# Block inversion of a chunked DeltaNet as a side chain on GpSimd, the gate-sum row in the decay buffer, norms by squares

## The chip, the cores and the metric

The kernel runs on one core of a Trainium2 chip. The metric is the device time of one execution in microseconds, as the median of several runs.

## The reference, cut to what matters

A decoder layer over 16 meta tokens and 512 positions, D = 2048, all float32:

```
xn = rmsnorm(h); proj = xn @ w_in                       # 2048 x 14368
u, z_pool, q, k, v, z, b, a, gate_pool, gate_dn = split(proj)
y_pool = (trailing_means(u) - u) @ mix * scale * silu(z_pool)
q, k, v = silu(causal_conv4(q, k, v)); q = l2norm(q) / sqrt(128); k = l2norm(k)   # 16 heads of 128
per head, chunks of C positions, decay[c, s] = exp(gcum[c] - gcum[s]) for s <= c:
    L = strict_lower(beta * (k @ k.T) * decay);  T = inverse(I + L)
    u_c = T @ (v * beta);  w_c = T @ (k * beta * exp(gcum));  qk = lower(q @ k.T * decay)
    for each chunk:  v_new = u_c - w_c @ S;  o = (q * exp(gcum)) @ S + qk @ v_new
                     S = S * g_last + (k * decay_to_end).T @ v_new
y_dn = rmsnorm(o) * silu(z)
merged = sigmoid(gate_pool) * (y_pool @ w_pool_out) + sigmoid(gate_dn) * (y_dn @ w_dn_out)
out = rmsnorm(h + merged @ w_o), meta positions dropped
```

## The kernel before, in words

**The projection** is the bulk. It is made in blocks of 256 output columns: 8 for the pooling branch, then 4 for each of 8 pairs of heads (k, q, v, z), then 16 for the merge gates. A block is a Strassen product of seven (`ORDER`), each cut in two chunks, so 14 chunks of 12 matmuls (`block_products`, L701); a float32 product is three float32r terms (high times high, high times low, low times high). For each chunk, in a ring of four slots, ScalarE copies the rounded weights (`split_hi`: `wh`, L1026) and VectorE subtracts to get the rest (`split_lo`: `wl`, L1475), three chunks ahead of TensorE (`AHEAD`). VectorE also makes four weight sums a block (`s1` to `s4`; `s2`, L1486, adds slots RE and RF and is made at chunk step t = 0 of its block), evicts the product sums (`c21`, `c22` at L1531, `c11`) and convolves. SyncE loads the weights: `block_loads` issues slots RA, RC, RF and RB of the next block, RF when VectorE has finished chunk 10 of this one. TensorE's last product in a block waits for `c22`, its last but one for `c21`.

**The side work.** While pair p is projected, the DeltaNet of pair d = p - 1 is run in between: `delta(d, m)`, 53 steps, one at each of certain hooks inside the blocks (`delta_step`: step m sits at hook 15*m//8 of the pair's 112, 28 a block). Each engine runs its own part of a step in its own instruction order, so a wait inside a step holds the projection work behind it on that engine. Named steps: G0 = 3 (Gram products of k into PSUM banks `pg`), F0 = 5 (Gram times decay into `mk`), V0 = 9 (transposes of v), W0 = 14 (inversion), L0 = 29 (blocks of the inverse are merged by matmuls), R0 = 35 (recurrence over four chunks of 128), O0 = 47 (normalise, transpose, gate). All loops over pairs are hardware loops (`Fori`) on TensorE, ScalarE, VectorE and GpSimd.

**The parts that the change touches.**
- Row load: GpSimd waits until the pair's output has been stored from `zst` (the same memory as `tm`; L2180), loads the cumulative gate row spread over 128 partitions into `tm` (L2164, L2166), subtracts each position's own sum into `dec` (L2175, L2176); VectorE then caps it (L1807) and ScalarE takes the exponential (L1189).
- Norms of k: VectorE multiplies the Gram banks by the identity into `st` (L1813, L1816), reduces (L1819, L1820), ScalarE takes the root (L1193). Norms of q: eight TensorE transposes of q into PSUM bank `pt` in two rounds (W0 + 2, W0 + 4), ScalarE squares with an accumulator (L1216).
- Inversion: `mk` (512 KB) is scaled (L1836; it is then complete, `mk_ready`), stored to DRAM (L1196, L1197), its 66 diagonal blocks of 16 x 16 come back one to a partition in `st` (L1219); VectorE inverts them by 14 steps of two dependent operations over 14 to 56 elements (L1855, L1858), copies a transposed form (L1861); two stores (L1224), and three loads bring block-diagonal matrices back into `tm` and `st` (L1227 to L1229). These DMAs are issued by ScalarE at fixed steps. TensorE's step L0 waits for `tm_loaded`.
- `load_vch` (SyncE) waits for `dec_diff`. `yraw` (the branch outputs for the last stage, 5 MB of its 6) is loaded in one DMA (L568) after all weight loads of the projection.

## Time and profile before

| | |
|---|---|
| median of 3 runs | 2041.04 us (2039.75 to 2042.32) |
| profiled execution, its own time | 2038.36 us |
| its span from first to last instruction | 2036.8 us |
| mean granted TensorE clock | 0.968 of 2.4 GHz |
| TensorE busy | 1862.6 us, 91% |
| VectorE busy | 1435.5 us, 70% |
| ScalarE busy | 953.8 us, 47% |
| GpSimd busy | 70.3 us, 3% |

Execution time is 1.6 us more than the span. The seven loop iterations and the last pair lie between about 446 us and 1330 us, each some 126 us long; the gate blocks follow to about 1560 us, and the two last stages to the end. PE is TensorE, PEld its weight load, DVE VectorE, ACT ScalarE, POOL GpSimd, SP SyncE; a small q behind a name is the engine's own queue of DMA issues and waits. Durations overlap a little where an engine starts an instruction before the one ahead has ended.

### The profile page before, as it was taken

Reading aid. Unit: us, or ns where it says so; the run is one execution under the profiler, and the core shown is the slowest. Engines: PE = TensorE matmul, PEld = TensorE weight load, DVE = VectorE, ACT = ScalarE, POOL = GpSimd, SP = SyncE. Lnnn points to the kernel's source line nnn. Section 1 sums busy time; section 2 is a strip of 40 time slices with the busy share of each in tenths; the row PEclk is TensorE's granted clock in tenths of the full one; section 3 lists DMA queues with packets and bytes.
Section 4 is the critical chain, followed back from the end, with each engine's and each line's share of the span. In section 5 each row is a group of like instructions: output and inputs, shape, how many; then the busy total and the mean of one; then the engine's idle time right before and its main releaser. Section 6 shows DMA issues by size and latency. Waiting matters only on the chain.

```text
span 2036.8 us, 40992 instructions
## 1 busy us (share of the span) xinstructions
PE 1862.6 (91%) x15073; PEld 1741.3 (85%) x15073; DVE 1435.5 (70%) x2628; ACT 953.8 (47%) x2148; POOL 70.3 (3%) x94
## 2 busy tenths in 40 slices
PE   5899999898988989888898898999997899999998
PEld 4889999888887888878888898899997688888886
DVE  7867799878778788787887878677776544335332
ACT  5544446455454554545555456455555322224222
POOL 2000010000000000000000000000000000000000
PEclk8999999899999999999999899999998999999999
DMA  5334355443454434544444355354546443437312
GB/s 151 84 83 110 108 152 163 115 138 99 121 150 113 147 97 113 151 112 148 108 112 151 101 152 135 88 144 128 141 124 217 145 136 122 153 107 260 125 37 83
DMA packets 355651, 260.93 MB, mean 128 GB/s; under 512 B 36865, under 2 KB 315866, under 8 KB 354794
## 3 DMA queue, kind: packets, MB, share of 16 engines
q1 hardware_dynamic: 283954, 197.35, 33.4%
q10 hardware_dynamic: 65160, 39.94, 6.8%
q0 software_dynamic: 6336, 21.08, 3.0%
q8 instruction: 113, 1.85, 0.4%
q14 instruction: 88, 0.72, 0.1%
HBM read 216.82 MB, written 42.60 MB: 127 GB/s over the span
## 4 chain that ended last, share of the span: by engine, by line
PE 62%; DVE 16%; issue 9%; DMA 6%; ACT 4%; ACTq 2%; DVEq 1%; SPq 0%; POOLq 0%; POOL 0%
PE pj L701 34%; PE pj L666 16%; PE pg L666 9%; DVE wl L1475 4%; PE pt L666 3%; DMA branch_scratch<-tm 2%; DVE stg L1796 2%; ACT wh L1026 2%; DMA tm<-gate_sum_scratch 2%; DMA yraw<-branch_scratch 1%; DVE st L1855 1%; DVE st L1858 1%; DVE raw L1508 1%; DVE raw L1499 1%; PE pt L832 1%
## 5 line engine op out<-in xcount | busy, mean ns | idle before, releaser
L701 PE MATMUL pj<-xh,wh 128*128 128x256 f32 (+2 forms) x3136 | 936.1, 299 | 92.9 <-DVE wl L1475 42.4
L701 PE MATMUL pj<-xl,wh 128*128 128x256 f32 (+2 forms) x3136 | 903.0, 288 | 0.0
L701 PE MATMUL pj<-xh,wl 128*128 128x256 f32 (+2 forms) x3136 | 901.6, 288 | 0.0
L1026 ACT ACTIVATE wh<-raw 128x512 fp32r<-128x512 f32 x784 | 484.9, 629 | 605.8 <-PE pj L701 423.7
L701 PEld LDWEIGHTS pj<-xh,wh 128*128 128x128 f32 x3136 | 611.1, 195 | 112.4 <-issue 54.0
L1475 DVE TENSOR_TENSOR wl<-raw,wh 128x512 fp32r<-128x512 f32 x784 | 534.8, 687 | 193.4 <-ACT wh L1026 187.6
L701 PEld LDWEIGHTS pj<-xl,wh 128*128 128x128 f32 x3136 | 612.6, 195 | 1.0 <-issue 1.0
L701 PEld LDWEIGHTS pj<-xh,wl 128*128 128x128 f32 x3136 | 609.9, 194 | 0.0
L666 PE MATMUL pj<-yh,bwh 128*128 128x512 f32 x384 | 149.8, 390 | 1.4 <-DVE yl L2010 1.4
L666 PE MATMUL pj<-yl,bwh 128*128 128x512 f32 x384 | 149.4, 389 | 0.0
L666 PE MATMUL pj<-yh,bwl 128*128 128x512 f32 x384 | 149.4, 389 | 0.0
L1026 ACT ACTIVATE bwh<-rawb 128x256 fp32r<-128x256 f32 x192 | 64.8, 405 | 175.1 <-PE pj L666 168.8
L2005 DVE TENSOR_TENSOR bwl<-rawb,bwh 128x256 fp32r<-128x256 f32 x192 | 69.1, 420 | 93.1 <-ACT bwh L1026 93.1
L1796 DVE SCALAR_TENSOR_TENSOR stg<-xin,convcur,stg 128x528 f32<-128x528 f32 x144 | 111.2, 773 | 0.0
L1486 DVE TENSOR_TENSOR raw<-raw 128x1024 f32<-128x1024 f32 x56 | 68.3, 1220 | 31.0 <-issue 30.9
L666 PEld LDWEIGHTS pj<-yh,bwh 128*128 128x128 f32 x384 | 72.1, 188 | 17.9 <-DVE yl L2010 3.0
L666 PEld LDWEIGHTS pj<-yh,bwl 128*128 128x128 f32 x384 | 72.1, 188 | 15.1
L666 PEld LDWEIGHTS pj<-yl,bwh 128*128 128x128 f32 x384 | 72.1, 188 | 14.6
L1493 DVE TENSOR_TENSOR raw<-raw 128x1024 f32<-128x1024 f32 x56 | 68.4, 1222 | 3.7
L1499 DVE TENSOR_TENSOR raw<-raw 128x1024 f32<-128x1024 f32 x56 | 68.2, 1218 | 2.1
L1508 DVE TENSOR_TENSOR raw<-raw 128x1024 f32<-128x1024 f32 x56 | 68.1, 1216 | 0.8 <-DMA raw<-in_w_in 0.8
L1026 ACT ACTIVATE snap<-pj 128x256 f32<-128x256 f32 (+2 forms) x168 | 62.1, 370 | 1.1 <-DVE ub L1531 0.2
(284 smaller groups left out, 1986.0 us busy)
## 6 DMA issues: line engine op xcount, KB each, us to landing
raw<-in_w_in SPq DMA_DIRECT2D x224, 512.0 KB, 4.1
head_scratch<-stg ACTq DMA_DIRECT2D x64, 264.0 KB, 2.8
rawb<-in_w_dn_out SPq DMA_DIRECT2D x16, 1024.0 KB, 6.2
rawb<-in_w_o SPq DMA_DIRECT2D x12, 1024.0 KB, 5.2
kq<-head_scratch SPq DMA_DIRECT2D x8, 1056.0 KB, 8.4
gates_scratch<-stg ACTq DMA_DIRECT2D x32, 256.0 KB, 3.5
rawb<-in_w_pool_out SPq DMA_DIRECT2D x8, 1024.0 KB, 5.2
yraw<-branch_scratch SPq DMA_DIRECT2D x1, 5120.0 KB, 20.6
```

What stands on the lines that cost most here:

```text
L666: return pe.matmul(dst, lhs, rhs, start=start, stop=stop)
L701: mm = pe.matmul(bank[:, c0:TH], w[:, slot, k, :], xx[what][:, kt, c0:TH], start=opens and one and kt == 0, stop=closes and last and kt == ...
L832: mm = pe.transpose(pt[rows, i * P:(i + 1) * P], src, ident)
L1026: return act.activation(dst, src, ACT.Copy)
L1475: tt(wl[:, slot, :, :], raw[:, SLOT_OF[what], HK * half:HK * (half + 1), :], wh[:, slot, :, :].bitcast(F32), ALU.subtract).then_inc(lo_don ...
L1486: tt(raw[:, RE, :, :], raw[:, RE, :, :], raw[:, RF, :, :], ALU.add).then_inc(sum_done, 1)
L1493: tt(raw[:, RF, :, :], raw[:, RC, :, :], raw[:, RF, :, :], ALU.add).then_inc(sum_done, 1)
L1499: tt(raw[:, RB, :, :], raw[:, RB, :, :], raw[:, RE, :, :], ALU.add).then_inc(sum_done, 1)
L1508: tt(raw[:, RE, :, :], raw[:, RA, :, :], raw[:, RC, :, :], ALU.add).then_inc(sum_done, 1)
L1796: dve.scalar_tensor_tensor(acc, xin[:, src_tap:src_tap + T], w, acc, ALU.mult, ALU.add).then_inc(conv_step, 1)
L1855: tt(own, wblk[:, 0:j, j:j + 1].broadcast_to([NBLK, j, rest]), gblk[:, j:j + 1, j + 1:BS].broadcast_to([NBLK, j, rest]), ALU.mult).then_in ...
L2005: tt(bwl[:, u, 2 * q:2 * q + 2, :], rawbs[u][:, 2 * q:2 * q + 2, c * P:(c + 1) * P], bwh[:, u, 2 * q:2 * q + 2, :].bitcast(F32), ALU.subtr ...
```

## The change

The inversion with all its DMAs goes from ScalarE and VectorE to one function on GpSimd, `inversion(d)`; the order there is inversion of pair d, row of pair d + 1, output store of pair d, and GpSimd's loop is written out. The row is loaded straight into `dec`, once the last product that reads `dec` of the pair before is done. Norms: ScalarE squares k and q at steps 0 and 1, and TensorE multiplies the squares by a column of ones (18 products of one column at step G0 + 1). `s2` of the next block moves from its step 0 to step 9 of the block before (14 in the first). `load_vch` waits for `y_stored` in place of `dec_diff`. The gate blocks' weight loads on SyncE are written out, and `yraw` comes in five loads of 1 MB behind the weight loads of gate blocks 6 to 10.

```diff
-                      V0 + 3: [("k", 8), ("k", 9), ("v", 8), ("v", 9)],
-                      W0 + 2: [("q", i) for i in range(0, 4)], W0 + 4: [("q", i) for i in range(4, 8)]}
+                      V0 + 3: [("k", 8), ("k", 9), ("v", 8), ("v", 9)]}
...
             def load_vch(d):
-                sp.wait_ge(dec_diff, d + 1)
+                need(sp, y_stored, 16 * d)
...
+            for i in range(4, NGATE):
+                block_loads(CP_GATE0 + i - 1, COL_GATE + i * CW)
+                if i == 6:
+                    sp.wait_ge(y_stored, 16 * PAIRS)
+                    sp.wait_ge(yp_stored, 16 * GROUPS)
+                if 6 <= i < 11:
+                    part = slice(4 * (i - 6), 4 * (i - 5))
+                    sp.dma_start(yraw[:, part, :], y_rows[:, part, :]).then_inc(yraw_loaded, 16)
...
+                    if h == 1:                                   # TensorE, step G0 + 1
+                        wait(norm_square, 2, 2)
+                        for at in range(NSLOT):
+                            cols = tokens(at % NCH) if at < SLOTS else slice(0, C)
+                            mm = product(pg[2][:, 64 + at:65 + at], squares_of[0][:, at // NCH if at < SLOTS else at - SLOTS, cols], one, True, True)
+                        for at in range(SLOTS):
+                            mm = product(pg[2][:, 64 + NSLOT + at:65 + NSLOT + at], squares_of[1][:, at // NCH, tokens(at % NCH)], one, True, True)
+                        mm.then_inc(norm_mm, 1)
...
+                if m < 2:                                        # ScalarE
...
+                    act.activation(squares_of[m], kq[:, m, :, :], ACT.Square).then_inc(norm_square, 1)
...
-                            act.activation(src, src, ACT.Square, accum_out=norms[:, 1, at:at + 1]).then_inc(tok_done, 1)
-                if m == F0 + 6:
-                    wait(mk_stored, 32, 32)
-                    act.dma_start(gblk, blocks(gram_d, 0, NBLK)).then_inc(blk_loaded, 16)
-                if m == W0 + 5:
-                    wait(w_turned, 1, 1)
...
-                if m == W0 + 10:
-                    wait(w_stored, 32, 32)
...
-                    if t == (3 if first else 0):                 # VectorE, block_steps
+                    if first and t == 3:
                         s2(b)
...
                     split_lo(b, par, t)
+                    if not last and t == (14 if first else 9):
+                        s2(b + 1)
...
+            def row_differences(d):                              # GpSimd
+                need(pool, qkv_mm, NCH * d)
+                pool.dma_start(dec[:, 0:XC], g_d[d:d + 1, 0:SLOTS, :].rearrange("a i c -> a (i c)").broadcast_to([P, XC])
...
+            def inversion(d):
+                pool.wait_ge(mk_ready, d + 1)
+                pool.dma_start(full_rows(gram_d), slots(mk)).then_inc(mk_stored, 16)
+                pool.dma_start(blocks(gram_d, NBLK - 2, NBLK).rearrange("a j c -> j a c"), tail(mk)).then_inc(mk_stored, 16)
+                pool.wait_ge(mk_stored, 32 * d + 32)
+                pool.wait_ge(norm_mm, d + 1)
+                pool.dma_start(gblk, blocks(gram_d, 0, NBLK)).then_inc(blk_loaded, 16)
...
+                for j in range(1, BS - 1):
...
+                    pool.tensor_tensor(own, wblk[:, 0:j, j:j + 1].broadcast_to([NBLK, j, rest]),
+                                       gblk[:, j:j + 1, j + 1:BS].broadcast_to([NBLK, j, rest]), ALU.mult).then_inc(w_prod, 1)
+                    pool.wait_ge(w_prod, done + j)
+                    pool.tensor_tensor(wblk[:, 0:j, j + 1:BS], wblk[:, 0:j, j + 1:BS], own, ALU.subtract).then_inc(w_step, 1)
...
+                for scratch, block_of in zip(inv_d, (wblk, wtr)):
+                    pool.dma_start(blocks(scratch, 0, NBLK), block_of).then_inc(w_stored, 16)
+                pool.wait_ge(w_stored, 32 * d + 32)
+                pool.wait_ge(tok_done, ALL_TOK * (d + 1))
+                pool.dma_start(slots(tm), full_rows(inv_d[1])).then_inc(tm_loaded, 16)
+                pool.dma_start(slots(st), full_rows(inv_d[0])).then_inc(st_loaded, 16)
+                pool.dma_start(tail(st), blocks(inv_d[0], NBLK - 2, NBLK).rearrange("a j c -> j a c")).then_inc(st_loaded, 16)
...
+            for d in range(PAIRS):
+                inversion(d)
+                if d < PAIRS - 1:
+                    row_differences(d + 1)
+                head_out(d)
```

## Rows read from the trace of the kernel before

**Rows 1.** Windows: stretch, us, busy (instructions) PE PEld DVE ACT POOL, clock, DMA share, GB/s.

```profile
1330.00:1550.00 220.00, 220.00 (x1861) 220.00 (x1861) 165.79 (x234) 120.57 (x224) 0.00 (x0) 1.00 0.50 132
...
826.00:952.00 126.00, 111.53 (x1118) 107.58 (x1117) 102.13 (x203) 65.25 (x162) 3.93 (x5) 0.96 0.45 125
...
876.00:881.00 5.00, 4.48 (x25) 4.48 (x26) 4.59 (x18) 2.95 (x15) 0.00 (x0) 0.66 0.57 159
...
883.50:890.00 6.50, 5.42 (x41) 4.78 (x40) 5.82 (x9) 3.78 (x7) 0.00 (x0) 1.00 0.24 39
```

**Rows 2.** Waits of TensorE in one pair, 827 to 953 us.

```profile
PE pt L832 <- ACT pt L1216: 3.1, 1, 3.1
PE pj L701 <- DVE xin L1531: 2.0, 1, 2.0
```

**Rows 3.** Timeline of TensorE in that pair: start, duration, instructions.

```profile
844.72 1.05 PE L666 MATMUL pg<-kq 128*128 128x128 f32 x8
845.61 0.60 PE L832 MATMUL pt<-cst,kq 128*128 128x128 f32 x4
...
876.52 0.66 PE L832 MATMUL pt<-cst,kq 128*128 128x128 f32 x4 [3.09 <-ACT pt L1216]
...
897.93 0.72 PE L666 MATMUL pg<-tm,mk 32*32 32x16 f32 x64
...
909.64 1.14 PE L666 MATMUL pg<-tm,mk 64*64 64x64 f32 x16
```

**Rows 4.** Timeline of ScalarE and its queue, 882 to 894 us.

```profile
883.42 1.67 ACT L1026 ACTIVATE wh<-raw 128x512 fp32r<-128x512 f32 x3 [4.47 <-PE pj L701]
...
893.18 1.15 ACT L1026 ACTIVATE wh<-raw 128x512 fp32r<-128x512 f32 x2 [3.49 <-issue]
```

**Rows 5.** Timeline of VectorE: the scaling of `mk`.

```profile
856.29 1.23 DVE L1836 TENSOR_TENSOR mk<-mk,qd 128x1024 f32<-128x1024 f32 x1 [0.27 <-DVE qd L1833]
```

**Rows 6.** Groups on VectorE, 860 to 896 us: count | busy us, mean ns | idle.

```profile
L1475 DVE TENSOR_TENSOR wl<-raw,wh 128x512 fp32r<-128x512 f32 x18 | 12.3, 687 | 4.9 <-ACT wh L1026 4.7
...
L1858 DVE TENSOR_TENSOR st<-st 66x14 f32<-66x14 f32 (+6 forms) x14 | 2.8, 197 | 0.5
```

**Rows 7.** GpSimd beside VectorE near 271 us, then GpSimd's smallest product by duration.

```profile
271.02 2.01 POOL L2175 TENSOR_TENSOR dec<-tm,table 128x1024 f32<-128x1024 f32 x1 [6.75 <-DMA tm<-gate_sum_scratch]
273.00 0.69 POOL L2176 TENSOR_TENSOR dec<-tm,table 16x32 f32<-16x32 f32 x1
...
271.19 2.41 DVE L1796 SCALAR_TENSOR_TENSOR stg<-xin,convcur,stg 128x528 f32<-128x528 f32 x1
...
L2176 POOL TENSOR_TENSOR dec<-tm,table x8: 228/229/690, 273.0 to 1220.4; 16x32 f32<-16x32 f32 x8
```

**Rows 8.** DMA issues, KB each, median us from issue to landing.

```profile
raw<-in_w_in SPq DMA_DIRECT2D x224, 512.0 KB, 4.1
...
gram_scratch<-mk ACTq DMA_DIRECT2D x8, 512.0 KB, 3.3
...
st<-inverse_scratch ACTq DMA_DIRECT2D x8, 512.0 KB, 7.1
...
branch_scratch<-tm POOLq DMA_DIRECT2D x8, 512.0 KB, 7.6
...
gate_sum_scratch<-grow POOLq DMA_DIRECT2D x1, 40.0 KB, 1.8
```

**Rows 9.** Groups of GpSimd's queue: what one DMA issue takes (mean ns).

```profile
L2198 POOL DMA_DIRECT2D gst<-gates_scratch x16 | 8.6, 540 | 376.3 <-DMA gates_scratch<-stg 273.3 <-DVE merged L2030 102.6
L2180 POOL DMA_DIRECT2D branch_scratch<-tm x8 | 6.0, 746 | 935.6 <-DVE tm L1946 935.6
```

**Rows 10.** Timeline of a gate block on VectorE around its steps 6 and 10.

```profile
1542.16 0.69 DVE L1475 TENSOR_TENSOR wl<-raw,wh 128x512 fp32r<-128x512 f32 x1
...
1547.61 0.41 DVE L1531 TENSOR_TENSOR stg<-snap,pj 128x256 f32<-128x256 f32 x1
```

**Rows 11.** Timeline of ScalarE where `yraw` lands.

```profile
1569.07 1.15 ACT L1026 ACTIVATE yh<-yraw 128x512 fp32r<-128x512 f32 x2 [13.31 <-DMA yraw<-branch_scratch]
```

More of the change, by code:

```diff
@@ L101 @@
 CODD = CEPS + 1
-NCONST = CODD + 1
+CONE = CODD + 1
+NCONST = CONE + 1
 CU, CONES = NCONST, NCONST + P
@@ L168, in build @@
         odd = cst[:, CODD:CODD + 1]
+        one = cst[:, CONE:CONE + 1]
         normw = vcol[:, 0:KT]
@@ L559, in _ @@
                 block_loads(CP_GATE0 + k - 1, COL_GATE + k * CW, ("kq", "v", None, "z")[k])
-            with sp.Fori(2, NGATE // 2) as i:
-                for k in range(2):
-                    block_loads(CP_GATE0 + 2 * i + k - 1, COL_GATE + i * (2 * CW) + k * CW)
-            sp.wait_ge(y_stored, 16 * PAIRS)
-            sp.wait_ge(yp_stored, 16 * GROUPS)
-            y_rows = y_d.rearrange("(k p) t -> p k t", p=P)
-            sp.dma_start(yraw[:, 0:20, :], y_rows[:, 0:20, :]).then_inc(yraw_loaded, 16)
+            y_rows = y_d.rearrange("(k p) t -> p k t", p=P)
+            for i in range(4, NGATE):
[6 more added lines that the diff above has]
+                    sp.dma_start(yraw[:, part, :], y_rows[:, part, :]).then_inc(yraw_loaded, 16)
             def load_b(jp, first, units=range(3)):
@@ L829, in delta @@
                         cols = slice(0, META) if n is None else tokens(n)
-                        src = vch[:, h, cols] if what == "v" else kq[:, "kq".index(what), h, cols]
+                        src = vch[:, h, cols] if what == "v" else kq[:, 0, h, cols]
                         rows = slice(0, META) if n is None else slice(0, P)
@@ L1185, in wait @@
                     need(act, semaphore, d * per_pair + count)
+                if m < 2:
+                    if m == 0:
+                        wait(kq_loaded, 16, 16)
+                        wait(tr_mm, NCH, 0)
+                    else:
+                        wait(o_tr, 2, 0)
+                    act.activation(squares_of[m], kq[:, m, :, :], ACT.Square).then_inc(norm_square, 1)
                 if m == 2:
@@ L1191, in delta @@
                 if m == F0:
-                    wait(norm_sum, 1, 1)
-                    act.activation(rk[:, 0, :], norms[:, 0, :], ACT.Sqrt, bias=eps).then_inc(norm_sqrt, 1)
-                if m == F0 + 2:
-                    wait(mk_ready, 1, 1)
-                    act.dma_start(full_rows(gram_d), slots(mk)).then_inc(mk_stored, 16)
-                    act.dma_start(blocks(gram_d, NBLK - 2, NBLK).rearrange("a j c -> j a c"), tail(mk)).then_inc(mk_stored, 16)
+                    wait(norm_mm, 1, 1)
+                    act.activation(rk[:, 0, :], pg[2][:, 64:64 + NSLOT], ACT.Sqrt, bias=eps).then_inc(norm_sqrt, 1)
+                    act.activation(norms[:, 1, 0:SLOTS], pg[2][:, 64 + NSLOT:64 + NSLOT + SLOTS], ACT.Copy).then_inc(norm_kept, 1)
                 if m in TOK_ROUNDS:
@@ L1212, in delta @@
                             act.activation(ktok[:, at, :], src, ACT.Copy, scale=cur[:, EDEC, at:at + 1]).then_inc(tok_done, 1)
[L1213 removed]
+                        else:
                             act.activation(vtok[:, at, :], src, ACT.Copy, scale=rk[:, 0, at:at + 1]).then_inc(tok_done, 1)
[L1215 to L1229 removed]
                 if m == L0 + 3:
@@ L1909, in delta @@
                         if n == 0:
-                            wait(tok_done, ALL_TOK, META_TOK)
+                            wait(tok_done, ALL_TOK, ALL_TOK)
                         for h in range(2):
@@ L2168, in _, with head_out @@
+            def head_out(d):
+                pool.wait_ge(y_ready, 2 * d + 2)
+                pool.dma_start(y_d[PW + CW * d:PW + CW * (d + 1), :].rearrange("(h e) t -> e h t", e=P), zst).then_inc(y_stored, 16)
             pool.wait_ge(gsum_stored, 16)
             pool.wait_ge(tab_dve, 6)
-            def row_differences(d):
-                row_load(d)
-                pool.wait_ge(rowg_loaded, 32 * d + 32)
-                own = table[:, bass.ds(d, 1), GCUM, :].rearrange("p a n -> p (a n)")
-                pool.tensor_tensor(slots(dec), slots(tm), bc(own[:, 0:SLOTS], C), ALU.subtract)
-                pool.tensor_tensor(tail(dec), tail(tm), bc(own[0:META, SLOTS:], META), ALU.subtract).then_inc(dec_diff, 1)
```

87 lines of the change are left out of this document (29 added, 58 removed).

## The prediction

> **What bounds the kernel now.** I read the windows first. In the gate blocks TensorE never stops: 1861 matmuls in 220 us, 0.118 us each at a granted clock of 1.00, the 2.4 GHz level [rows 1]. That is the rate at which a block costs nothing but itself. A pair's iteration has the same four blocks, 672 matmuls or 79 us, and lasts 126 us [rows 1]. So 47 us a pair are side work, waits and slow clock, and the change can only take from these. VectorE is busy 102 of the 126 us, TensorE 112 [rows 1]; neither is full, yet each waits in order for the other. GpSimd is nearly idle.
>
> The waits of TensorE in one pair then say which ends last [rows 2]. Apart from the jump of the hardware loop, which all engines show and which stays, the two longest are these: 3.1 us are the second round of q transposes, which waits for ScalarE to square the first round out of the same bank. 2.0 us are a wait for VectorE's `c22` (L1531). Each has a cause in side work that the change moves. Before the q round ScalarE had reached its squares late, at 876 us; the matmuls behind the hold then run at clock 0.66, so partly at the 1.2 GHz level [rows 1, 3]. The `c22` wait goes back to ScalarE's queue: it stood in the inversion's store step before the `wh` at 883.42, and later sat 3.49 us behind its DMA issues with the next `wh` not made [rows 4].
>
> **The change part by part**, per pair, TensorE's path as the measure.
>
> Norms of q. The 8 transposes go: 0.60 us recorded for four, 0.2 of it the pipeline's end under the next instruction [rows 3], so 0.8 us in all. The hold goes, 3.1 us [rows 2]. Behind it 4.48 us were busy for 21 main matmuls and 4 transposes, which at 0.118 would be 2.9 us: 1.6 us more [rows 1]. Together 5.5 us.
>
> ScalarE's waits for the inversion and its DMAs. From 883.5 to 890 us 41 matmuls took 6.5 us where 4.8 would do, because `wh` came at 883.42 after an idle 4.47 us [rows 1, 4]: 1.7 us. The second block of issues: 2.0 us [rows 2, 4]. Together 3.7 us. What else could hold TensorE in these places is VectorE, which loses 28 operations of 0.197 us a pair [rows 6], and about half as much again for the diagonal products, so I count both as gone.
>
> Norms by ones. 18 float32 products are 36 passes with full 128 x 128 weights and one column. No such row exists. Above: a Gram pass, 0.89 us for 8 (844.72 to 845.61) or 0.111 each, gives 4.0 us. Below: a 64 x 64 pass, 1.14 us for 16 or 0.071, gives 2.6 us [rows 3]. The weights are full size and the columns few, so I take 3.0 us, added to the path. ScalarE's two squares replace sixteen small instructions and lie at the head of the iteration, where TensorE is still working off its ring.
>
> So TensorE would come to step L0 5.5 + 3.7 - 3.0 = 6.2 us sooner, at 891.7 instead of 897.93 us in this pair [rows 3]. `mk` is complete at 857.6 [rows 5], and I leave that where it is: the sums on VectorE go, but F0 now waits for the ones products behind the Gram products. **The side chain has 34 us** before TensorE waits for it at L0, with the whole projection queued behind that wait.
>
> The chain on GpSimd, step by step. An issue on its queue takes 0.54 us with 128 runs and 0.746 us with 256 [rows 9]. The stores and loads here have about 1024 runs (8 slots x 128 rows, or 66 blocks x 16 rows). Below: 0.75 us if the runs don't matter. Above: by the slope between the two rows, 0.75 + 768 x 0.0016 = 2.0 us. I take 1.2, nearer the measured rows.
> - Gram store: 1.2 and 0.5 for its tail, then landing. ScalarE's same store landed in 3.3 us, GpSimd's 512 KB store took 7.6 beside other traffic [rows 8]. 5.0 us (4 to 8).
> - Block load, 66 KB: 1.2 and some 2.3; the 40 KB store took 1.8 [rows 8]. 3.5 us (2.5 to 6).
> - 28 steps. GpSimd's smallest product takes 0.229 us alone [rows 7], so 28 are 6.4 us; with larger shapes and the three other operations 7.7 us, the lower end. But at 273.00 the same product took 0.69 us, and ended only with VectorE's operation at 273.6; and that VectorE operation, begun at 271.19, had itself taken 2.41 us and ended 0.6 us after GpSimd's long one, about one operation of its own later [rows 7]. The two keep each other out. If each step waits for one VectorE operation, 28 x 0.69 and 1.5 make 21 us, the upper end. Between 860 and 896 us VectorE has 28 such operations with two operands in its memory, 18 of them `wl` of 0.687 us [rows 6], some 20 of 36 us: about half of GpSimd's steps wait, (14 x 0.25) + (14 x 0.69) and 1.5 for the others are 14.7; I take 13.5, since VectorE loses work.
> - Two stores: 2.4 and 2.1 us, 4.5 (3.3 to 7).
> - Three loads: ScalarE's took 7.1 us for the later of the two large ones [rows 8]. 7.5 us (6 to 10).
>
> The sum is 34.0 us (23.5 to 52): just what there is. The SBUF — State Buffer page of the Trainium skill (Who interferes with whom) speaks against this move: it says that a VectorE operation with two SBUF inputs and a GpSimd operation that reads SBUF exclude each other for a whole instruction. The rows near 271 us agree; by the rule taken alone, with VectorE never pausing, the steps would take the 21 us of the upper end and the chain 41.5 us.
>
> With the spread I charge 1.5 us of waiting at L0, slow clock behind it included (1.6 us followed the 3.1 us hold, [rows 1]).
>
> `s2` moved to step 9. It needs slot RF, issued after step 6 of the same block (about 1542.8 us) and landing 4.1 us later [rows 8, 10]; `s2` would then run from 1546.9 to 1548.1, and `c22`, done at 1548.0 before, at 1549.1 [rows 10]. TensorE needs it about then. In a gate block that is nothing to 0.5 us, 2 us over all of them; in a pair, with more traffic and a fuller VectorE, 1.0 us for its four blocks (0 to 3). The gain, an earlier start behind the loop's jump, I put at nothing, since TensorE starts from its full ring.
>
> Row load into `dec`. It starts once `qkv_mm` is done, some 20 us before it is needed, so VectorE's wait for `dec_diff` goes. TensorE had no idle time there, so nothing; 1 us at most. It stands behind the inversion on GpSimd and ahead of the output store, and both are idle by then. `load_vch` waits for `y_stored`, which comes earlier than its turn on SyncE: nothing, 0.5 us if that slips, in front of RF.
>
> `yraw` early. ScalarE waited 13.31 us for the 5 MB load, and with it VectorE's `wl`, so the last block stood [rows 11]. The five loads of 1 MB go into gate blocks where the DMA engines are half idle (0.50, [rows 1]). Behind the wait VectorE alone sets the pace, so the whole tail moves: 13.3 us (10 to 15), once.
>
> **Sum.** Per pair 9.2 - 3.0 - 1.5 - 1.0 = 3.7 us, for 7 iterations and the last pair 30 us. Then 13.3, less 2 for the gate blocks: 41 us. From the profiled execution's own 2038.36 us (span 2036.8 and 1.6 around it) this gives 1997; the median of the runs lies 2.7 us above that execution, so **2000 us**.
>
> **The rivals.**
> - *The chain is late.* Slower, by one mechanism: TensorE stands at L0 until `tm_loaded`. Each us past 34 costs 8 us. It decides from a chain of about 39 us: 41 us gained over 8 pairs are 5.1 a pair. At 44 us (the exclusion nearly full, issues at 1.6 us) TensorE waits 10 and pays 1.5 for the clock, so 9.2 - 3.0 - 11.5 - 1.0 = -6.3 a pair, 50 us worse, less 11: 2080 us. For it: VectorE's 102 of 126 us and 273.00. Against: small steps hardly delay VectorE, and half its time is free of them.
> - *The chain is hidden and VectorE's relief counts.* Chain under 32, norms at 2.6, `s2` free, 1 us gained at the other waits for `wl`: 9.2 - 2.6 + 1.0 = 7.6 a pair, 61 us and 13: 1967 us.
> - *The waits only change names.* ScalarE's and the q holds go, but `s2` before `c22` and VectorE's delays behind GpSimd cost 3 us more a pair: 3.7 - 3 = 0.7, 6 us and 11: 2024 us.
> - *`yraw` alone helps*, the chain being some 37 us: about 2025 us as well. That nothing changes needs the gain of `yraw` to be just cancelled; no mechanism aims there.
>
> **How the numbers follow.** Forecast (1983 to 2012) 0.38; hidden chain (below 1983) 0.16; waits renamed or a chain of 35 to 38 us (2012 to 2037) 0.15; within 0.2% of before, about what a measurement can tell from no change (2037 to 2045), 0.04; late chain (above) 0.27. Faster is 0.69, same 0.04, slower 0.27. The likeliest case's own range is 1983 to 2012. Leaving out a tenth on either side, the range goes from 1962 to 2072.
>
> **What the profile after would show.** No wait of `pt` for L1216; 18 one-column products at about 0.08 us a pass; GpSimd's 28 steps over 10 to 18 us, some of them 0.2 and some 0.7 us; the last load landing 30 to 38 us after `mk` is scaled; at L0 no TensorE wait above 3 us; no 13 us wait before the first `yh`; `c22` waits under 1 us. It would be wrong if TensorE's longest wait in a pair is at L0, or if GpSimd's DMA issues take 2 us or more.

## The result, and the profile after

The changed kernel takes 2108.1 us in the median of four runs (2101.8 to 2115.3), the kernel before 2041.7 us beside it: a ratio of 1.033 (95% interval 1.028 to 1.037), 66 us slower where I had forecast 41 us faster. The profiled execution took 2115.3 us, its span 2113.8, at a mean granted clock of 0.945 (0.968 before) and with GpSimd busy 276 us (70 before); what follows is read from it, so its differences add up to 77 us.

The windows come first. I cut them where VectorE evicts `c22` (L1530), once a block. The first row is the gate blocks, then the four intervals of one pair, to be held against its 126.1 us before; before, these four took 34.9, 31.0, 33.6 and 26.6 us. The ones products lie in the first interval, the third is that of L0.

```profile
1410.00:1630.00 220.00, 218.29 (x1823) 216.11 (x1823) 162.65 (x230) 118.22 (x218) 0.74 (x1) 1.00 0.56 158
...
879.20:917.60 38.40, 35.12 (x260) 34.70 (x260) 20.36 (x36) 20.46 (x45) 2.48 (x3) 0.87 0.40 117
917.60:940.42 22.82, 20.97 (x171) 20.35 (x169) 20.52 (x31) 13.36 (x26) 19.59 (x33) 1.00 0.43 116
940.42:984.27 43.85, 35.11 (x493) 33.22 (x494) 28.91 (x57) 12.88 (x32) 2.82 (x4) 0.84 0.38 101
984.27:1015.41 31.14, 27.94 (x226) 26.66 (x224) 26.82 (x46) 18.86 (x46) 4.72 (x5) 1.00 0.44 134
```

The pair takes 136.2 us, 10 more. The interval ahead of L0 lost 8.2 us, which is the relief that I had looked for, and more of it; the interval of L0 gained 10.2, the one with the ones products 3.5, the last 4.5. From `c22` to `c22` over the whole run: 8.0 us more up to the end of the first pair's own blocks, beside which no DeltaNet runs, 80 in the eight stretches with one (331 to 1329 us before), 4.0 in the eleven plain gate blocks (20.2 us each in place of 19.9), 14.2 less in the last block (24.0 in place of 38.2, where `yraw` was waited for), 1.0 less behind it. That sums to 77.

TensorE's waits in this pair (873.4 to 1009.8 us; us in total, times, longest):

```profile
PE pg L668 <- DMA tm<-inverse_scratch: 7.6, 1, 7.6
PE pj L703 <- issue: 2.7, 1, 2.7
PE pj L703 <- DVE stg L1530: 2.4, 1, 2.4
PE pj L703 <- DVE xin L1530: 2.2, 2, 1.9
```

The hold of the q transposes (3.1 us, [rows 2]) is gone. In its place stand a wait of 7.6 us at L0 for the end of the side chain, and three waits for `c22` (2.4, 1.9 and 0.3 us) in place of one. Then the chain itself, on GpSimd's timeline:

```profile
908.77 0.91 POOL L2144 DMA_DIRECT2D gram_scratch<-mk  x1 [34.61 <-DVE mk L1828]
...
914.63 1.06 POOL L2148 DMA_DIRECT2D st<-gram_scratch  x1 [4.43 <-DMA gram_scratch<-mk]
...
927.96 0.63 POOL L2163 TENSOR_TENSOR st<-st 66x56 f32<-66x56 f32 x1
928.67 0.64 POOL L2160 TENSOR_TENSOR st<-st 66x56 f32<-66x56 f32 x1
929.39 0.62 POOL L2163 TENSOR_TENSOR st<-st 66x56 f32<-66x56 f32 x1
930.09 0.64 POOL L2160 TENSOR_TENSOR st<-st 66x54 f32<-66x54 f32 x1
930.80 1.16 POOL L2163 TENSOR_TENSOR st<-st 66x54 f32<-66x54 f32 x1
...
937.29 0.22 POOL L2160 TENSOR_TENSOR st<-st 66x14 f32<-66x14 f32 x1
```

VectorE's timeline over the same microseconds:

```profile
927.65 0.78 DVE L1474 TENSOR_TENSOR wl<-raw,wh 128x512 fp32r<-128x512 f32 x1
928.35 0.80 DVE L1797 SCALAR_TENSOR_TENSOR stg<-xin,convcur,stg 128x528 f32<-128x528 f32 x1
929.08 0.78 DVE L1474 TENSOR_TENSOR wl<-raw,wh 128x512 fp32r<-128x512 f32 x1
929.78 0.79 DVE L1797 SCALAR_TENSOR_TENSOR stg<-xin,convcur,stg 128x528 f32<-128x528 f32 x1
930.50 1.31 DVE L1498 TENSOR_TENSOR raw<-raw 128x1024 f32<-128x1024 f32 x1
```

The two are in lockstep. GpSimd's step of 928.67 ends at 929.31, a little behind VectorE's of 928.35, which ends at 929.15; that of 930.80 ends at 931.96, again behind the long sum of 930.50. A step beside `wl` or a convolution takes 0.62 us, beside a sum of 1.31 us it takes 1.16, and with VectorE idle at 937.29 it takes 0.22. Of the 28 steps 22 take 0.37 to 1.26 us and six take 0.21 to 0.26, three of these at the end: nearly four in five are held up, not half of them. VectorE pays too: `wl` 0.78 in place of 0.69.

TensorE's timeline around the ones products and at L0, then the same places in windows:

```profile
894.18 1.25 PE L668 MATMUL pg<-kq 128*128 128x128 f32 x12
895.36 2.39 PE L668 MATMUL pg<-cst,st 128*128 128x1 f32 x20
897.61 2.48 PE L668 MATMUL pg<-cst,mk 128*128 128x1 f32 x16
899.96 1.09 PE L842 MATMUL pt<-cst,kq 128*128 128x128 f32 x4
...
951.01 1.05 PE L668 MATMUL pg<-tm,mk 32*32 32x16 f32 x64 [7.64 <-DMA tm<-inverse_scratch]
```

```profile
897.50:899.90 2.40, 2.40 (x19) 2.40 (x19) 0.00 (x0) 0.00 (x0) 0.00 (x0) 0.77 0.00 0
899.90:905.50 5.60, 5.60 (x27) 5.60 (x28) 2.72 (x5) 3.79 (x9) 0.00 (x0) 0.50 0.00 0
944.00:951.00 7.00, 0.00 (x0) 0.02 (x1) 1.74 (x4) 0.00 (x0) 2.33 (x3) 0.68 0.84 219
951.00:960.50 9.50, 9.49 (x236) 8.88 (x236) 5.29 (x13) 2.07 (x4) 0.00 (x0) 0.51 0.10 27
```

From 895.36 to 899.96 are 4.6 us for 36 passes, 0.128 each on the mean: from start to start the first 30 take 0.112 us, as a Gram pass does, and the last ones 0.213. The granted clock falls inside them to 0.50, the 1.2 GHz level, although TensorE has no gap in the records, and 27 matmuls behind them take 5.6 us where 3.2 would do at full clock. At L0 it falls during the wait and stays low for 9.5 us more.

### The profile page after: what moved, and what is told of

It reads as the page before. It is cut to its first block, busy times and chain, and to the rows that moved or that the text cites. A ratio compares the mean times of both kernels' runs of the same rounds, so it can differ in the third digit from the quotient of the medians.

```text
span 2113.8 us, 40951 instructions
## 1 busy us (share of the span) xinstructions
PE 1922.7 (91%) x15297; PEld 1797.2 (85%) x15297; DVE 1386.8 (66%) x2340; ACT 956.6 (45%) x2044; POOL 276.1 (13%) x405
## 4 chain that ended last, share of the span: by engine, by line
PE 59%; DVE 12%; DMA 11%; issue 8%; POOL 7%; ACT 3%; DVEq 1%; ACTq 0%; SPq 0%; POOLq 0%
PE pj L703 28%; PE pj L668 17%; PE pg L668 11%; DVE wl L1474 4%; DMA raw<-in_w_in 3%; POOL st L2163 3%; POOL st L2160 3%; PE pt L668 2%; DMA inverse_scratch<-st 2%; DMA tm<-inverse_scratch 2%; DMA gram_scratch<-mk 2%; DMA st<-gram_scratch 1%; ACT wh L1036 1%; DVE raw L1507 1%; DVE stg L1797 1%
## 5 line engine op out<-in xcount | busy, mean ns | idle before, releaser
L1474 DVE TENSOR_TENSOR wl<-raw,wh 128x512 fp32r<-128x512 f32 x784 | 550.1, 705 | 281.9 <-ACT wh L1036 248.5
L703 PEld LDWEIGHTS pj<-xh,wh 128*128 128x128 f32 x3136 | 618.6, 197 | 119.8 <-DVE wl L1474 55.6
L703 PEld LDWEIGHTS pj<-xl,wh 128*128 128x128 f32 x3136 | 620.5, 198 | 1.0 <-issue 1.0
L703 PEld LDWEIGHTS pj<-xh,wl 128*128 128x128 f32 x3136 | 618.5, 197 | 0.0
L1485 DVE TENSOR_TENSOR raw<-raw 128x1024 f32<-128x1024 f32 x56 | 69.2, 1237 | 61.4 <-DMA raw<-in_w_in 61.4
L668 PE MATMUL pg<-tm,mk 32*32 32x16 f32 (+2 forms) x896 | 25.0, 215 | 58.5 <-DMA tm<-inverse_scratch 58.5
L668 PEld LDWEIGHTS pg<-tm,mk 32*32 32x32 f32 (+1 forms) x896 | 22.4, 144 | 63.1 <-issue 62.1
L1036 ACT ACTIVATE snap<-pj 128x256 f32<-128x256 f32 (+2 forms) x168 | 62.5, 372 | 25.0 <-DVE xin L1530 14.3
L1492 DVE TENSOR_TENSOR raw<-raw 128x1024 f32<-128x1024 f32 x56 | 68.5, 1222 | 4.5
```

Source lines behind the costliest of these rows:

```text
L668: return pe.matmul(dst, lhs, rhs, start=start, stop=stop)
L703: mm = pe.matmul(bank[:, c0:TH], w[:, slot, k, :], xx[what][:, kt, c0:TH], start=opens and one and kt == 0, stop=closes and last and kt == ...
L1036: return act.activation(dst, src, ACT.Copy)
L1474: tt(wl[:, slot, :, :], raw[:, SLOT_OF[what], HK * half:HK * (half + 1), :], wh[:, slot, :, :].bitcast(F32), ALU.subtract).then_inc(lo_don ...
L1485: tt(raw[:, RE, :, :], raw[:, RE, :, :], raw[:, RF, :, :], ALU.add).then_inc(sum_done, 1)
L1492: tt(raw[:, RF, :, :], raw[:, RC, :, :], raw[:, RF, :, :], ALU.add).then_inc(sum_done, 1)
```

## The experiments

All times are medians; the kernel before lay between 2042 and 2045 us beside them, so differences of a few us between kernels that were measured at different times mean little. "Pair" is the median distance from one pair's last `c22` to the next one's in the profile, without the first, which is shorter in every kernel. "First interval", "ahead of L0", "L0" and "last interval" are the four of a pair, cut as above.

### Each part undone in the changed kernel

`s2_back`, `chain_back`, `norms_back` each restore one part as it was before; `yraw_alone` is the kernel before with the five early loads.

```diff
-                    if first and t == 3:                         # s2_back
+                    if t == (3 if first else 0):
                         s2(b)
-                    if not last and t == (14 if first else 9):
-                        s2(b + 1)
...
-                inversion(d)                                     # chain_back: old code on ScalarE, VectorE
...
-                        wait(norm_square, 2, 2)                  # norms_back: old code at G0, W0 + 2, W0 + 4
...
-            sp.dma_start(yraw[:, 0:20, :], y_rows[:, 0:20, :]).then_inc(yraw_loaded, 16)   # yraw_alone
+                    sp.dma_start(yraw[:, part, :], y_rows[:, part, :]).then_inc(yraw_loaded, 16)
```

> The kernel after, with s2 back at step 0 of its own block and nothing else changed. After's trace has the eleven c22 intervals of the pooling blocks and the first pair's k 6.3 us longer in all than before's, the gate blocks 0.3 us each, and TensorE's waits for c22 50 us in place of 21. Theory A (the move of s2 costs far more than the 1.0 us a pair of my forecast, because VectorE now stands in its order before s2 until slot RF has landed, and c22 and the splits stand behind it): 6 for the first blocks, 3 to 4 a pair and 4 for the gates come back, so 2108 goes to about 2070 (2060 to 2085). Theory B (the c22 waits only collect lateness that the GpSimd chain and the slow clock make): it stays within 10 us, 2098 to 2108.

Measured 2089.4 us, 19 less: between the two. Without the stall of `s2` TensorE comes to L0 sooner and waits longer for the chain there, 90.4 us in place of 58.5 over the eight pairs, so the chain took much of the rest:

```profile
PE pg L668 <- DMA tm<-inverse_scratch: 90.4, 8, 12.6
```

> The kernel after, with the inversion back on VectorE and its DMAs back on ScalarE's queue at their old steps; norms, row, s2 and yraw stay new. Theory A (the chain of some 42 us is what sets a pair's length: TensorE waits 7.6 us at L0 in each pair and pays for the clock after it): the 7.6 and some 1.5 come back, ScalarE's 3.7 are lost again, so 5 us a pair, about 2068 (2055 to 2080). Theory B (the wait at L0 only collects time that would be lost at another place, the ones products and s2 being the cause): the time stays at 2095 to 2110.

2087.2 us, 21 less; neither. The wait at L0 is gone, but TensorE's waits for `wl` (330 to 1360 us) are 42.9 us where the changed kernel had 5.9.

> The kernel after, with the old norms (diagonal of the Gram banks on VectorE, eight transposes of q squared by ScalarE). Theory A (the 36 one-column passes cost 4.6 us a pair and the granted clock falls with them, some 2.5 us more, while the q transposes' hold would hide in the 7.6 us that TensorE waits at L0 anyway): 6 to 7 us a pair come back, about 2055 (2045 to 2070). Theory B (the clock falls for another reason and the norms are a fair exchange, 4.6 for 5.5): within 10 us of 2108.

2057.8 us, 50 less, within theory A. Undone in the changed kernel, the norms are the part that gives most back.

> The kernel before, with only the five early loads of the branch outputs in place of one late one. Theory A (as forecast, and as after's trace has it, where the last projection block takes 24.0 us between its c22 and the one before in place of 38.2): 13 to 14 us faster, 2027 to 2029. Theory B (the early loads slow the gate blocks' weight loads; their blocks took 20.2 us in place of 19.9 in the kernel after): 4 to 5 us are given back, 2032.

2028.4 us, 14 less than before. Theory A: the forecast's 13.3 us are there, and the gate blocks stay at 19.9 us. The 0.3 us more in the changed kernel are thus not the early loads; they are the move of `s2`, since they are gone in `s2_back` (19.9 us) too.

### Each part alone

The other corners of the cube: row, `load_vch` and `yraw` stay new, and of `s2`, norms and chain none or one is new.

> The kernel after with s2, the norms and the whole inversion back, so of the change only the row loaded into the decay buffer, the other wait of load_vch and the early branch outputs are left. Theory A (the row costs and gains nothing, as forecast): the time of the early branch outputs alone, 2028 (2024 to 2031). Theory B (the row's place ahead of the output store on GpSimd, or load_vch's wait, holds the pair's loads): 2035 or more.

2039.9 us (2017.8 to 2047.7): theory B by the number, with a mechanism that neither had. VectorE's and GpSimd's timelines show it:

```profile
830.32 0.68 DVE L1479 TENSOR_TENSOR wl<-raw,wh 128x512 fp32r<-128x512 f32 x1
830.92 2.41 DVE L1800 SCALAR_TENSOR_TENSOR stg<-xin,convcur,stg 128x528 f32<-128x528 f32 x1
```

```profile
830.63 2.13 POOL L2173 TENSOR_TENSOR dec<-dec,table 128x1024 f32<-128x1024 f32 x1 [5.21 <-DMA dec<-gate_sum_scratch]
```

The subtraction now runs some 20 us earlier in the pair, 10 us ahead of `c22` and no longer behind it, beside VectorE's work, and a convolution of 0.76 us takes 2.41, in each of seven pairs. The interval goes from 26.5 to 28.0 us, 1.5 us a pair or 10 in all. But the row gives as much back: the first intervals take 10 us less in all, 6.6 of them in the last DeltaNet (26.9 in place of 33.5). There, in `yraw_alone` (1223.5 to 1257 us), the old row load had waited for the output store, VectorE for the row, and TensorE for what hung on it:

```profile
DVE dec L1807 <- POOL dec L2176: 7.5, 1, 7.5
POOL tm L2164 <- DMA branch_scratch<-tm: 7.5, 1, 7.5
...
PE pt L832 <- ACT ktok L1212: 5.6, 1, 5.6
```

So in the profiles the row as such comes out even, within a few us. For the 11 us between the two medians, and for the spread, the granted clock (below) is the likely cause, but for the 11 us that isn't shown. `load_vch`'s wait was not tested apart from the row.

> As the run before this one in the list, with the inversion chain on GpSimd: norms and s2 are old, the chain alone is new. Theory A (it is late by itself: in the kernel after with the old norms TensorE still waited 6 us a pair at L0, and without the s2 stall it comes there sooner): L0 waits 8 to 10 us a pair, the q transposes' hold and ScalarE's 3.7 us are hidden or gone, net 1 to 2 us a pair slower than the row and branch outputs alone, 2040 (2034 to 2048). Theory B (alone it is hidden, and only the later mk_ready of the ones products made it late): the 3.7 us of ScalarE's queue come back, 2000 (1992 to 2010).

2046.2 us, pair 129.6: theory A. TensorE waits 83.2 us at L0, 10.4 a pair, and the interval ahead of L0 is 23.0 us in place of 30.7. The chain is late by itself.

> As the first, with the new norms alone; inversion and s2 are old. Theory A (the one-column passes cost 4.6 us and 2.5 us of slow clock after them, against 5.5 us for the q transposes and their hold): 1 to 2 us a pair slower, 2040 (2034 to 2046). Theory B (the slow clock came from somewhere else): 1 us a pair faster, 2020 (2012 to 2026).

2052.8 us, pair 130.5: worse than either. The first interval went from some 34.1 to 38 us; the one in which the q transposes' hold stood stayed at 30.6. TensorE's waits from 330 to 1360 us say why:

```profile
PE pj L704 <- DVE wl L1492: 45.4, 50, 2.1
```

With the q transposes there these waits were 16.6 us. The hold of 23.2 us went, and 28.8 of waits for `wl` came.

> As the first, with s2 at step 9 alone; inversion and norms are old. Theory A (nothing absorbs its stall here, while 19 us came back by undoing it in the kernel after, where the wait at L0 took the rest): 30 to 38 us slower, 2062 (2055 to 2070). Theory B (my forecast's 1.0 us a pair and 2 for the gates, what more was seen being the chain's doing): 2038 (2032 to 2044).

2051.4 us, pair 128.4: between. Some 9 us up to the end of the first pair's blocks and 0.3 a gate block; in a pair the last interval takes 3 us more (31.0) and the first 2 less (some 32), a gain that the forecast had put at nothing.

The whole cube, by what is new (`yraw` and row always): none 2039.9, chain 2046.2, s2 2051.4, ones 2052.8, chain and s2 2057.8, s2 and ones 2087.2, chain and ones 2089.4, all 2108.1 us. The parts alone cost 6, 12 and 13 us; together 68. An obvious reading is that terms hide behind each other: the ones products stand ahead of `mk`, so they delay the chain's start as much as TensorE's way to L0, while the q transposes that they replace stood between `mk` and L0. The intervals of the profiles show that little of the 68 us comes from this. Summed over the eight DeltaNets, the first interval grows by 36 us with the ones products where neither other part is new, by 37 with `s2` or with the chain beside them, and by 50 with both: in three of four cases the same, some 4.5 us a pair. What differs most is the interval of L0, and in it the time at half clock (granted clock 0.50):

| new (sums of eight, us) | L0 intervals | of that at half clock |
|---|---|---|
| none | 298 | 68 |
| s2 | 282 | 24 |
| ones | 274 | 20 |
| s2 and ones | 282 | 38 |
| chain | 362 | 85 |
| chain and ones | 380 | 119 |
| chain and s2 | 333 | 65 |
| all | 353 | 113 |

The corner "none" is thus itself slowed by falls of the clock at L0, and the others look cheap beside it: its fastest run, 2017.8 us, is 22 us below its median. The 23 us that `s2` and ones cost beyond their sum all lie in the L0 column. For chain and ones, against the chain alone, the wait at L0 grows by only 7 us (90.4 in place of 83.2) and the interval ahead of it even shrinks by 12; the rest of the 18 us more at L0 is slow clock. These are single profiles, and why the clock falls more often at L0 in one kernel than in another isn't shown.

### The ones products

`ones_twice` makes the 18 products twice. `ones_wide` makes them with 16 columns of ones.

```diff
-                        for at in range(NSLOT):                  # ones_twice
+                        for at in 2 * list(range(NSLOT)):
...
-        one = cst[:, CONE:CONE + 1]                              # ones_wide, NW = 16
+        one = cst[:, CONE:CONE + NW]
```

> The kernel after, with the 18 products of the squares by the column of ones made twice (36 more passes a pair, same result). Theory A (they cost their 4.3 to 4.6 us and make the granted clock fall, and mk waits for them, so that the chain starts later by all of it and nothing is absorbed at L0): 6 to 8 us a pair more, 2108 goes to 2160 (2152 to 2172). Theory B (the passes cost their own time alone, the clock falls for other reasons): 4.5 us a pair, 2144 (2138 to 2150).

2168.6 us, 60 more, 7.6 a pair: theory A. Its timeline of TensorE shows the clock falling inside the streak:

```profile
917.46 5.33 PE L668 MATMUL pg<-cst,st 128*128 128x1 f32 x40
922.65 6.96 PE L668 MATMUL pg<-cst,mk 128*128 128x1 f32 x32
```

The first 33 passes take 0.112 us each, the other 39 0.213. In windows of 1 us the clock is 1.00 up to 921 us, 0.50 from 922 to 934.

> The kernel after, with 16 columns of ones in place of one in its 36 passes, of which one is read. Theory A (the granted clock falls because one-column passes leave the array nearly unused, though the records show TensorE busy; a pass lasts as long as its weight load either way): the fall behind them, 7 us at half clock in the kernel after, shrinks or goes, 2 to 3 us a pair, 2108 goes to 2088 (2080 to 2098). Theory B (the fall is not theirs, or a pass costs more with 16 columns): 2104 to 2115.

2105.5 us, 3 less: theory B within the noise. A pass with 16 columns lasts as long as with one (20 in 2.3 us); the fall behind them lasted 3 us in the pair that I looked at, but the first intervals, 37.1 to 40.2 us, are close to those of the changed kernel (36.2 to 41.0). So that the few columns make the clock fall is not shown; what is shown is that it falls in or right behind these passes at either width.

### Where the relief went

`steps_on_vector` is the changed kernel with the arithmetic back on VectorE and the chain's DMAs left on GpSimd; `dmas_on_pool` is `yraw_alone` with only these DMAs moved. The row is old in the latter. `dmas_late1`, `2` and `3` are `dmas_on_pool`, and `chain_late5` is `only_chain`, with L0 and all behind it so many delta steps later. `q_left_out` is `yraw_alone` and `relief_both` is `dmas_late2`, each without the norms of q: the output is scaled with 1 in their place.

```diff
+            def inversion_dmas(d):                               # GpSimd, behind row_differences(d)
+                pool.wait_ge(mk_ready, d + 1)
+                pool.dma_start(full_rows(gram_d), slots(mk)).then_inc(mk_stored, 16)
...
+                pool.dma_start(gblk, blocks(gram_d, 0, NBLK)).then_inc(blk_loaded, 16)
+                pool.wait_ge(w_turned, d + 1)                    # VectorE's steps at W0, as before
...
-        L0 = W0 + 15                                             # dmas_late1, 2, 3; chain_late5
+        L0 = W0 + 18                                             # + 16, 17 and 18; 20 in chain_late5
...
+                need(sp, qs_mm, NCH * d)                         # load_kq
```

> The kernel after, with the 31 arithmetic steps of the inversion back on VectorE in its old five delta steps, while all DMAs of the chain stay on GpSimd's queue. Theory A (on GpSimd each step lasts as long as the VectorE operation beside it, 20.6 us for all; on VectorE they take some 10, so the chain is 10 us shorter and the 7.6 us at L0 go, clock included, for some 4 us of VectorE's time): 4 to 5 us a pair faster, 2070 (2060 to 2080). Theory B (VectorE paces the blocks, as its waits for wl in the kernel with the whole inversion back show): no better than that kernel, 2087 (2082 to 2092).

2091.0 us: theory B. The loads are issued earlier and nothing is waited for at L0, yet it is no faster than with the whole inversion back; waits for `wl` are 36.4 us.

> The kernel before with the early branch outputs, and of the move to GpSimd only the seven DMA issues and their waits; the arithmetic stays on VectorE, norms, s2 and row are old. Theory A (my forecast's term for ScalarE's waits, 3.7 us a pair, is right): 2028 goes to 1998 (1992 to 2006). Theory B (VectorE's own order paces these blocks, and the holds of ScalarE come back as waits for wl, as the holds of the q transposes did): 2028 (2020 to 2034).

2028.4 us, exactly the time without the move: theory B by the number. But the intervals say something else: the one ahead of L0 is 27.0 us in place of 30.7 and TensorE's waits for `c22` (14.0 us in all) are gone, so the relief of 3.7 us was there; the one of L0 is 37.4 to 39.5 us in all eight, where `yraw_alone` has 33.7 to 35.9 in five and 39.7, with 14 us at half clock, in three. TensorE's timeline there:

```profile
893.59 0.47 PE L666 MATMUL pg<-st,work 32*16 32x16 f32 x35
897.42 0.37 PE L666 MATMUL pg<-st,work 32*16 32x16 f32 x28 [3.36 <-issue]
```

It stops for 3.4 us between two of 64 equal products, with no semaphore between them, and by 2.9 to 3.7 us in each of the eight, 26.0 in all. In the kernel before, the same place has 0.7 us in this pair, at most 1.1 in the other six of the loop, and 3.5 in the last DeltaNet, which lies outside the loop.

> The kernel with the DMAs alone on GpSimd, with L0 and all behind it two delta steps (some 4 us) later, and the load of k and q waiting for their last use. Theory A (the 3.4 us stop is tied to the moment at which L0 comes, right behind the landing of the loads and with its small products close together; later it goes): the block before keeps its 27 us, that of L0 comes back to 34, so 2028 goes to 2000 (1992 to 2008). Theory B (it belongs to these small products wherever they stand, or VectorE has not caught up): 2024 to 2032.

2013.8 us, halfway. The stop is gone in seven of the eight, a good pair takes 123.1 us (33.5 at L0), a pair's last interval 29.0 in place of 26.5.

> As the kernel with the DMAs alone on GpSimd and L0 two delta steps later (2014 us), with one step in place of two. Theory A (a pair's last block grows by 1.2 us for each step, since the delta's tail moves into it, and one step is enough to lose the stop): 2006 (2000 to 2012). Theory B (the stop comes back at this place): 2018 to 2028.

2019.2 us (2007.8 to 2030.8): theory B. The stop is 1.7 us on the mean (13.7 over the eight pairs, longest 2.4), and the last interval is already 28.1.

> The same with three steps. Theory A (only the tail grows): 1.2 us a pair more than with two, 2022 (2016 to 2028). Theory B (more room for the clock and for VectorE at L0): 2013 or less.

**1997.7 us**, ratio to before 0.9765 (0.973 to 0.980): theory B, and faster than both kernels. In windows, the interval of L0 of one pair, then the one ahead of L0 and that of L0 of the next, and one whole pair:

```profile
876.00:911.92 35.92, 34.27 (x486) 32.34 (x485) 27.56 (x52) 12.65 (x26) 0.00 (x0) 0.86 0.44 125
974.45:1001.49 27.04, 23.38 (x180) 22.50 (x179) 25.41 (x63) 15.63 (x42) 4.38 (x5) 0.94 0.43 97
1001.49:1034.63 33.14, 31.49 (x486) 29.92 (x485) 27.57 (x52) 12.65 (x26) 0.00 (x0) 0.95 0.48 137
911.92:1034.63 122.71, 111.97 (x1119) 107.73 (x1118) 104.25 (x203) 66.18 (x161) 10.91 (x13) 0.96 0.46 128
```

2028.4 to 1997.7 is 3.8 us a pair, but that it equals the forecast's 3.7 is in part luck. Against `yraw_alone`, summed over the eight, the intervals ahead of L0 take 29 us less, which is the 3.7 a pair; those of L0 25 less and the last ones 23 more, since side work has moved from the one to the other and the clock falls less often at L0 (34 us at half clock in place of 55); and the first ones 12 less. L0 later with the DMAs left on ScalarE was not run, so how much of the gain the move of L0 gives alone stays open.

> The kernel before with the early branch outputs and without the norms of q: the eight transposes and the squares are left out, the output's scaling uses the constant 1 for them. Theory A (my forecast's term: transposes, hold and slow clock are 5.5 us a pair): 2028 goes to 1984 (1978 to 1992). Theory B (the hold of 3.1 us only takes the place of waits for wl, since VectorE paces that block, as block and waits in the kernel with the new norms alone show): 0 to 1.5 us a pair, 2020 (2014 to 2030).

2023.3 us: theory B. Not transposing q at all is worth 5 us at most, 0.6 a pair, and that isn't clear of noise: against the kernel before, both this kernel and `yraw_alone` have a ratio of 0.991. The intervals ahead of L0 stay at 30.5 to 30.9 us; waits for `wl` grow from 11.5 to 43.1 us.

> The one before with the norms of q left out as well (constant 1 in their place). Theory A (with both holds gone the path of TensorE is what counts, and the forecast's 9.2 us a pair are there): 1955 to 1970. Theory B (VectorE's order is the pace): not below 2000.

2013.1 us, that of `dmas_late2`: theory B. The q norms are worth nothing there either.

> The kernel with the chain alone on GpSimd (old norms, old s2), with L0 and all behind it five delta steps later, some 10 us, and the load of k and q waiting for their last use. Theory A (the lateness at L0, 10.4 us a pair, is all that the chain costs; the block before L0 had become 8 us shorter): 7 to 8 us a pair come back, 2046 goes to 1985 (1975 to 2000). Theory B (VectorE and the exclusion pace the pair, and the time saved at L0 appears as waits for wl): 2030 to 2046.

2028.0 us, 18 less than with L0 in its place: nearer B. L0 still waits 42.9 us in all, and the last interval grew from 28.0 to some 32.1 us, with 20.2 us of waits for VectorE's scaling of the output (`mk`, L1907) where `only_chain` had 7.3.

## Why the prediction was wrong

The sign is wrong: 3.7 us gained a pair in the forecast, 10 lost in the profile. Three steps of the sum failed: half of GpSimd's steps waiting (13.5 us; 22 of 28 do, 20.6), the ones products at 3.0 us and without the clock (4.6, and 2.4 of slow clock behind them), and the hold of the q transposes counted as 5.5 us of gain (0.6 at most). Of the rivals, the late chain was the right one in its mechanism and its place; its price was not, since other terms fell too.

- **Late chain: available time right by luck, length wrong.** `mk` was complete at 908.5 us and TensorE stood at L0 from 943.4: 34.9 us, forecast 34. The forecast let the ones products delay L0 by 3.0 us but not `mk`, though they stand ahead of both, and set 9.2 us of relief between `mk` and L0, where 5.4 came (40.3 us before). From its first issue the chain took 42.2 (to 951.0), forecast 34.0. By terms: Gram store 5.9 (5.0), block load 3.6 (3.5), steps 20.6 (13.5), stores 7.2 (4.5), loads 5.0 (7.5). The step that failed is "about half of GpSimd's steps wait": I had worked out 21 us for all waiting, had the row at 273.00 that showed it, and argued it down with VectorE's half-free time. But each step depends on the one before and starts 0.07 to 0.08 us behind it, and that one ends a little behind a VectorE operation, when VectorE has just started its next: the two fall into step. Here the rule of the Trainium skill (SBUF — State Buffer, Who interferes with whom) would have given the 21 us and the 41.5 that I quoted beside it, and the trace agrees, 20.6 and 42.2; in the second, stores that took longer and loads that took less cancel. The large issues took 0.9 to 1.06 us, forecast 1.2.
- **Ones products.** 4.6 us, forecast 3.0 with 4.0 as its upper end; the upper bound was exact, since at full clock a pass with full weights takes 0.112 us with 1 column, with 16 and, in the Gram passes, with 128; I had gone below it on the strength of 64 x 64 passes. I had no term for the granted clock, 0.6 us inside the streak and 2.4 behind it: together 7, and 7.6 measured by doubling them. Net of the old norms of k, the first interval shows 4.5 us a pair where one of the other parts or none is new, and 6.2 in the changed kernel.
- **Norms of q.** I counted 5.5 us; `q_left_out` gives 0.6 at most. I had read the longest wait as the cost. VectorE's ring was the pace of that block, and the hold of 3.1 us merely stood where TensorE would have waited for `wl`: 23.2 us of holds went, and these waits grew by 31.6 (`q_left_out`) and 28.8 (`only_ones`). That is the rival "the waits only change names", for this term.
- **ScalarE's waits.** 3.7 us, and the interval ahead of L0 is 3.7 us shorter in `dmas_on_pool` and all kernels built on it. At the old place of L0 a stop of 3.4 us and slow clock took them; in the changed kernel the chain did.
- **`s2` at step 9.** Forecast 10 us in all. Alone 12, undone in the changed kernel 19, undone with the ones products alone beside it 34. Of the forecast's own terms: 0.3 us a gate block lies in its range for them (0 to 0.5) and sums to 4.0, twice the 2 that I took; the first blocks' 8 us I had left out. In the pair VectorE stood 1.88 and 2.21 us for slot RF, and TensorE 2.4 us for `c22` behind it, as the mechanism said.
- **Row load.** "Nothing; 1 us at most" a pair: in the profiles it comes out even, but as 10 us lost to the collision, 1.5 a pair, and 10 gained at other places. I looked at who waits for it and not at what runs beside it, though the convolution of 2.41 us at 271 us in [rows 7] was the same collision; and that TensorE had no idle time there doesn't hold for the last pair, where it waited 5.6 us.
- **`yraw`.** 13.3 forecast, 14.3 measured. The wait before the first `yh` (13.31 us, [rows 11]) is gone:

```profile
1647.12 1.14 ACT L1036 ACTIVATE yh<-yraw 128x512 fp32r<-128x512 f32 x2
```

Put together for a pair of the profile: 7.6 us at L0 and some 5 of slow clock behind it (9.5 us at half clock), 7 for the ones products, 1 to 3 for `s2` and 1.5 for the row, less the 8.2 by which the interval ahead of L0 shrank. That is 14 to 16 against 10 found; the terms overlap, as the first interval shows, which grew by 3.5 us only.

What stays open: what TensorE waits for in the stop of 3.4 us, and why the clock falls more often at L0 in one kernel than in another, on which the price of each part alone depends by up to 24 us.

## What to carry to other kernels

A long wait of the busiest engine is worth what remains when it is taken away: before counting it, see whether the engine that feeds it has any slack in that stretch, and try it by leaving the work out. Small dependent steps put on GpSimd beside a busy VectorE should be priced at one step per VectorE operation; here 22 of 28 ran so. Relief in one stretch (3.7 us a pair here) can be lost at the next fixed point behind it, so look at both intervals before calling a term wrong. And before parts are priced by leaving one out at a time, compare the time at half clock in their profiles.

## What the runs showed of the hardware

- **The same instructions at two clocks.** Two pairs of `yraw_alone`, the interval with L0's small products, in windows (the second row of each is the stretch behind them):

```profile
514.44:554.09 39.65, 37.23 (x492) 35.32 (x493) 28.87 (x58) 13.20 (x33) 0.00 (x0) 0.83 0.31 89
527.44:541.50 14.06, 14.06 (x115) 13.08 (x113) 6.80 (x14) 1.26 (x2) 0.00 (x0) 0.53 0.15 49
645.59:679.22 33.63, 31.34 (x492) 29.72 (x493) 28.73 (x57) 13.19 (x33) 0.00 (x0) 1.00 0.36 105
658.60:672.60 14.00, 14.00 (x163) 13.42 (x160) 12.22 (x23) 4.89 (x11) 0.00 (x0) 1.00 0.16 51
```

  In the first the granted clock fell to 0.50, the 1.2 GHz level, for 14 us, soon behind a wait of 1.40 us of TensorE for VectorE's `work`, and the interval took 6 us more; in the second the same wait was 1.12 us, and the clock stayed at 1.00. So kernels with this stage spread by some 6 us per fall. The ten runs of `only_row_yraw` show it: the fastest, 2017.8 us, has a mean granted clock of 0.973, the four from 2032.6 to 2037.0 have 0.965 to 0.970, and the slowest, 2047.7, has 0.960. So differences of 10 us between single profiles say little.
- **A fall without a gap.** The clock fell some 4 us after the start of a streak of one-column products that left no gap in TensorE's records (`ones_twice`), and the last 32 of them took 6.8 us in place of 3.6. The Trainium skill (TensorE: Matmul & The Clock Gate, What's actually happening) has the lower clock as that of an engine that has been idle; by that rule it would not have fallen here, and the measurement decides.
- **Mutual exclusion at full length.** An operation of GpSimd that takes 0.21 to 0.26 us where nothing holds it up took 0.62 beside a `wl` or a convolution and 1.16 beside a sum of 1.31 us (the changed kernel), and a 0.76 us convolution took 2.41 beside a subtraction of 2.13 us (`only_row_yraw`).
- **DMA issues on GpSimd** took 0.9 to 1.06 us with some 1000 runs, against 0.54 and 0.75 with 128 and 256 [rows 9]: far less than the 2.0 us that the slope between those two rows gives.
